# An S5 stage in another order, a layer-vector schedule with one knot moved, and two norm transposes one step earlier

## What is computed

```
def s5_mixer(h, w_in, ..., d_skip, w_glu):
    u = h @ w_in
    bu_r, bu_i = (u by group) @ bbr, (u by group) @ bbi
    _, _, s_r, s_i = associative_scan(combine, (a_r, a_i, bu_r, bu_i), axis=0)
    y = s_r @ c_re - s_i @ c_im + d_skip * u
    ya, yb = split(gelu(y) @ w_glu, 2)
    return ya * sigmoid(yb)

for layer in range(2):            # second network
    mod = silu(c) @ ada_w[layer] + ada_b[layer]      # shifts, scales, gates
    h = rms_norm(x) * g * (1 + sc1) + sh1
    x = x + g1 * mixer(h)
    x = x + g2 * conv_ffn(rms_norm(x) * g * (1 + sc2) + sh2)
    (the same for ctx)
```

## Time and profile before

| | us |
|---|---|
| median of 3 runs | 3034.11 |
| lowest, highest | 3031.2, 3043.46 |
| the profiled execution | 3034.11 |
| its span in the profile | 3032.3 |
| TensorE busy | 2926.8 |
| VectorE busy | 1806.9 |
| ScalarE busy | 1103.4 |
| GpSimd busy | 407.0 |

### The profile page before, as it was taken

One profiled execution on the slowest core, in us unless ns is written; L12 is line 12 of the kernel. 1 busy time (PEld: TensorE's weight loads), 2 busy tenths in 40 slices (PEclk: granted clock), 3 DMA queues, 4 the chain that ended last, 5 costly groups with the idle time before them and its releaser, 6 DMA issues. The chain is left out here.

```text
span 3032.3 us, 37645 instructions
## 1 busy us (share of the span) xinstructions
PE 2926.8 (97%) x15078; PEld 2437.5 (80%) x15078; DVE 1806.9 (60%) x2518; ACT 1103.4 (36%) x1571; POOL 407.0 (13%) x390
## 2 busy tenths in 40 slices
PE   6999988999999999999999999999999999999999
PEld 5778767788878778888768888889998886778887
DVE  7456546766666567776536586665764437554443
ACT  3233224333332442323324432234553426442322
POOL 0100111686642100001000000000000103100000
PEclk9999999999999999999989999999999999999999
DMA  6444322455638555554314365544553431123232
GB/s 268 145 134 139 105 97 78 147 179 171 225 127 268 169 180 170 160 166 148 118 50 139 111 188 180 181 153 126 181 175 100 133 95 51 38 84 99 96 97 84
DMA packets 123310, 421.00 MB, mean 139 GB/s; under 512 B 21520, under 2 KB 21520, under 8 KB 122368
## 3 DMA queue, kind: packets, MB, share of 16 engines
q1 hardware_dynamic: 102096, 369.67, 37.9%
q0 software_dynamic: 11056, 41.95, 4.2%
q10 hardware_dynamic: 9984, 6.97, 0.7%
HBM read 401.31 MB, written 19.86 MB: 139 GB/s over the span
## 5 line engine op out<-in xcount | busy, mean ns | idle before, releaser
L121 DVE TENSOR_TENSOR wl<-raw,wh 128x1024 fp32r<-128x1024 f32 x506 | 659.9, 1305 | 545.0 <-ACT wh L118 519.0
L112 PE MATMUL bk<-HH,wh 128*128 128x512 f32 x2176 | 862.3, 396 | 25.2 <-DVE HL L133 13.4
L112 PE MATMUL bk<-HL,wh 128*128 128x512 f32 x2176 | 854.8, 393 | 0.0
L112 PE MATMUL bk<-HH,wl 128*128 128x512 f32 x2176 | 854.3, 393 | 0.0
L118 ACT ACTIVATE wh<-raw 128x1024 fp32r<-128x1024 f32 x506 | 531.1, 1051 | 428.5 <-PE bk L112 421.2
L112 PEld LDWEIGHTS bk<-HH,wh 128*128 128x128 f32 x2176 | 413.8, 190 | 119.5 <-DVE HL L133 16.0
L112 PEld LDWEIGHTS bk<-HH,wl 128*128 128x128 f32 x2176 | 413.3, 190 | 87.5
L112 PEld LDWEIGHTS bk<-HL,wh 128*128 128x128 f32 x2176 | 414.2, 190 | 85.6 <-issue 1.0
L124 DVE CUSTOM_DVE_ANT_0 ttr<-ar,cB 128x1024 f32<-128x1024 f32 x240 | 309.9, 1291 | 2.2
L112 PE MATMUL bk<-gh,wh 128*128 128x512 f32 x704 | 274.3, 390 | 0.3 <-DVE gl L121 0.3
L112 PE MATMUL bk<-gh,wl 128*128 128x512 f32 x704 | 273.9, 389 | 0.0
(11 more groups left out here) (301 smaller groups left out, 3863.3 us busy)
## 6 DMA issues: line engine op xcount, KB each, us to landing
raw<-in_wts_dram SPq DMA_DIRECT2D x506, 512.0 KB, 3.6
ar<-in_ada_dram SPq DMA_DIRECT2D x176, 512.0 KB, 4.2
first<-in_ada_dram SPq DMA_DIRECT2D x16, 512.0 KB, 15.3
F_d<-CA POOLq DMA_DIRECT2D x8, 512.0 KB, 5.0
E_d<-stg POOLq DMA_DIRECT2D x16, 256.0 KB, 4.1
M_d<-K_d POOLq DMA_DIRECT2D x8, 512.0 KB, 11.7
EB<-E_d POOLq DMA_DIRECT2D x8, 512.0 KB, 6.6
EB<-M_d POOLq DMA_DIRECT2D x8, 512.0 KB, 7.1
```

The lines of the kernel that those rows point to most:

```text
L112: return Nothing() if self.e is None else self.e.matmul(*a, **k)
L121: return Nothing() if self.e is None else self.e.tensor_tensor(*a, **k)
```

## The change

There are four edits.

1. In S5, PE runs all eight tiles of `s5u` before `past(1)`, where two of them stood behind `past(1)` and `own(1)`. `out(0)` moves ahead of `past(2)`, and `own(2)` and `out(1)` ahead of `past(3)`. `LOADS` and the places of the fetches follow. On DVE the `lo` of units 139 and 140, which stood behind `scan(1)` and `scan(3)`, now both stand ahead of `scan(1)`.
2. In `KNOTS` the point (142, 78) becomes (138, 78), so the ten modulation steps due by unit 152 start at unit 140.
3. In `f2` the PE transpose `norm_turn(cf2)` moves from the start of up 3 to the start of up 2.
4. The same in the context FFN for `norm_turn(o)`.

```
-KNOTS = (... (122, 78), (142, 78), (152, 88), ...)
+KNOTS = (... (122, 78), (138, 78), (152, 88), ...)

-LOADS = [E0, E1, M0, M1, E2, E3, M2, M3, E4, E5, F0, F1,
-         F2, F3, E6, E7, M4, M5, M6, M7, F4, F5, F6, F7]
+LOADS = [E0, E1, M0, M1, E2, E3, M2, M3, F0, F1, E4, E5,
+         M4, M5, F2, F3, E6, E7, M6, M7, F4, F5, F6, F7]

 s5_pe:
             own(0)
-            for _ in range(2):
-                next(g)
+            run(g)
             past(1)
             own(1)
-            run(g)
+            out(0)
             past(2)
-            out(0)
+            own(2)
             out(1)
             past(3)
-            own(2)
             own(3)

 s5_vec:
             lo(e, base["s5u"] + 5 + 3)
+            lo(e, base["s5u"] + 7 + 3)
             scan(1)
-            lo(e, base["s5u"] + 6 + 3)
             scan(2)
             scan(3)
-            lo(e, base["s5u"] + 7 + 3)

 s5_pool:
-                for qr in {5: (0, 1), 10: (2,), 15: (3,)}.get(n, ()):
+                for qr in {5: (0, 1), 9: (2,), 10: (3,)}.get(n, ()):

 tensor_program:
-            ffn_pe(e, f2, lambda e, *key: norm_turn(e, n_cf2, 4) if key == ("up", 3) else None)
+            ffn_pe(e, f2, lambda e, *key: norm_turn(e, n_cf2, 4) if key == ("up", 2) else None)
-            ffn_pe(e, fc, lambda e, *key: norm_turn(e, n_o, 5) if key == ("up", 3) else None)
+            ffn_pe(e, fc, lambda e, *key: norm_turn(e, n_o, 5) if key == ("up", 2) else None)
```

More of the change, by code:

```diff
@@ L362, in build @@
         mm_ = Space()
-        KNOTS = ((0, 0), (2, 16), (12, 24), (58, 48), (76, 48), (122, 78), (142, 78), (152, 88), (214, 132), (222, 132), (240, 144), (260, 144), (318, 192), (600, 192))
+        KNOTS = ((0, 0), (2, 16), (12, 24), (58, 48), (76, 48), (122, 78), (138, 78), (152, 88), (214, 132), (222, 132), (240, 144), (260, 144), (318, 192), (600, 192))
         def mod_rate(u):
@@ L1293, in build @@
         d_yf = [landing("yf") for _ in range(8)]
-        LOADS = [("E", 0), ("E", 1), ("M", 0), ("M", 1), ("E", 2), ("E", 3), ("M", 2), ("M", 3), ("E", 4), ("E", 5), ("F", 0), ("F", 1),
-                 ("F", 2), ("F", 3), ("E", 6), ("E", 7), ("M", 4), ("M", 5), ("M", 6), ("M", 7), ("F", 4), ("F", 5), ("F", 6), ("F", 7)]
+        LOADS = [("E", 0), ("E", 1), ("M", 0), ("M", 1), ("E", 2), ("E", 3), ("M", 2), ("M", 3), ("F", 0), ("F", 1), ("E", 4), ("E", 5),
+                 ("M", 4), ("M", 5), ("F", 2), ("F", 3), ("E", 6), ("E", 7), ("M", 6), ("M", 7), ("F", 4), ("F", 5), ("F", 6), ("F", 7)]
         SLOT = {kind: n % 5 for n, kind in enumerate(LOADS)}
```

## The result

| | before | after |
|---|---|---|
| median, first comparison (6 runs each) | 3042.37 us | 3060.23 us |
| ratio | | 1.0061 [1.0040, 1.0083] |
| median, repeated on another chip (23 and 6 runs) | 3040.93 us | 3054.02 us |
| ratio | | 1.0051 [1.0034, 1.0067] |
| profiled execution / its span | 3034.11 / 3032.3 us | 3058.09 / 3056.3 us |

The change is slower by 0.5 to 0.6%: +17.9 us between the medians of the first comparison, +13.1 in the second. The ratio is worked out from all runs and is not the quotient of the medians; by it the two differences are 18.6 and 15.5 us. The forecast was 3050.0 us with a range of 3041 to 3057, made as 3034.1 + 15.9. The direction was right and the time lies outside the range.

What follows compares the result with a forecast made beforehand. The prediction took TensorE, busy 2926.8 of 3032.3 us, as the bound. It added 5.6 + 2.6 + 3.0 + 2.2 + 2.5 = 15.9 us to 3034.1, giving 3050.0 us, range 3041 to 3057.

Steps and rivals of the forecast that it cites:

- The wait in the latent FFN, 5.6 us: Latent FFN, start of up 2: TensorE stands still 5.6 us at the moved transpose until DVE's reciprocal is made.
- 5.6 + 2.6 = 8.2: Latent FFN: the 5.6 us stall at the moved transpose plus 2.6 us for the clock drop behind it.
- The wait in the context FFN, 3.0 us: Context FFN, start of up 2: TensorE waits 3.0 us at the moved transpose for the reciprocal.
- Its clock loss, 2.2 us: Context FFN, behind the transpose's wait: a clock drop costing 2.2 us, with 0 and 2.9 as the ends.
- Rival D: Both FFNs: the moved transposes do not wait, so only S5's loss is left, 3036.6 us; chance 0.06.
- S5, +2.5 us: S5: old waits go, but later scans and a new 4.0 us wait ahead of `past(2)` net +2.5 us.
- E4: S5: the load `past(2)` waits for, landing at 958.6, 960.9 or 965.2; middle case a new 4.0 us wait.
- The knot, 0: The moved `KNOTS` point: modulation steps run earlier on DVE, mostly beside dense matmuls of `glu`, costed at 0.
- The base, 3034.1 us: Whole kernel before: the profiled execution's 3034.1 us, also the runs' median, to which the predicted loss was added.
- Rival A: Both FFN stalls come, but the clock holds once or S5 comes out even: 3045, or 3047 to 3048; chance 0.22.
- Rival B: S5 becomes bound by its loads, +7 us there in place of +2.5: 3054.5 us; chance 0.12.
- Rival C: Not slower: the S5 order's 7.4 us gain pays for the two stalls' 8.6, giving +1.2 or 3035; chance 0.06.

Runs made afterwards that it cites:

- s5_warm2: Kernel before with only the new S5 order, plus 16, 4 and 10 useless matmuls ahead of `past(2)`, `own(2)` and `out(2)`: 3035.85 us, ratio 0.9989.
- no_knot: The changed kernel without the `KNOTS` edit, so the new S5 order and both moved transposes, against the kernel before: 3056.13 us, ratio 1.0051.
- old_warm10: Kernel before, old S5 order, with ten useless 512-column matmuls put ahead of `past(3)`: 3040.02 us against 3040.4, ratio 0.9990.
- turn_cf2: Kernel before with only the context FFN's transpose moved to the start of up 2: 3043.17 us against 3040.93, ratio 1.0006.
- s5_warm: Kernel before with only the new S5 order, plus 16 useless 512-column matmuls ahead of `past(2)`: 3037.38 us, ratio 0.9999.
- knot: Kernel before with only the `KNOTS` point moved, S5 order and transposes as before: 3042.35 us, ratio 0.9997.
- old_warm: Kernel before, old S5 order, with twenty useless 512-column matmuls put ahead of `past(3)`: 3032.26 us against 3040.93, ratio 0.9978.

## Why the forecast was wrong, step by step

*The wait in the latent FFN, 5.6 us:* right. It is 5.45, by the row named in the forecast, and 8.6 us with its clock loss, where 5.6 + 2.6 = 8.2 was said. In the traces the two come to 8.4, and the second drop behind the norm sums, 1.5 us that the forecast did not have, comes on top.

*The wait in the context FFN, 3.0 us:* right, 2.92. *Its clock loss, 2.2 us:* wrong in after, where PEclk stays at 1.00 behind this wait, which the forecast had named as a sign against itself; 1.7 us in the profile of edit 4 alone. Edits 3 and 4 cost 12.2 us by the runs where the forecast has 13.4, so the sum is nearer than its terms. Rival D is excluded.

*S5, +2.5 us:* the pieces were right: scan 1 at 951.2 (said 952.9), a wait ahead of `past(2)` of 3.63 us (said 4.0), the reason E4. That `z(3)` ends at 983.37 in `s5_warm2` (said 983.5) is partly luck, as scan 1 starts 1.4 us earlier there and 1.4 us of idle time come between the scans. (One reading is 0.1 us off: 955.00 + 1.06 - 953.36 is 2.7 and not 2.8.)

Wrong was the clock. The forecast read from the earlier trace rows that it loses 2.2 us behind a wait and is back within 4 to 6 us. In S5 the pieces behind the wait are small matmuls, and half clock lasted 17 to 48 us in the profiles of the new order without filler, and 34 to 37.5 in five of six of the old one. So `glu` starts at 996.72, where the forecast had `out(3)` end between 987 and 991. As a difference the term need not be wrong, since both orders lose the clock. In the traces S5 takes 10.5 us more in after than in before. Against the five other profiles of the old order (mean 199.9) the two of the change are 1.4 and 5.3 us longer. With the 12.2 us of edits 3 and 4 that is 13.6 to 17.5, near the 15.5 and 18.6 that the ratios give.

*The knot, 0:* right, 3042.35 against 3042.19, and `no_knot` no better than the change.

*The base, 3034.1 us:* this is the step that failed. It was the profiled execution and the median of three runs, of which one was 3043.46. In the comparison itself the median of before is 3042.37, and in four later ones it is 3040.4 to 3042.2. Of the 10.2 us by which 3050.0 missed 3060.2, 8.3 are the base and 2.0 the difference (17.9 against 15.9). The cause is the clock reading above: the forecast took a stage with 6.8 us at half clock as what before always does. The forecast's difference of 15.9 us, a ratio of 1.0052, lies in both measured intervals; put on 3041 to 3042 it gives 3057 to 3058. That this difference fits so well is partly luck: terms that were too high (the second clock loss) and one that was missing (the drop behind the norm sums) offset each other. What was missing is the question why the three runs were 12 us apart (3031.2 to 3043.46); the profiles of the old S5 order differ by 8 to 10 us in the length of that stage alone. The range should have taken in a base of up to 3043.

Rival A has the right pieces (the second drop partly absent), but not S5. Rival B said that E4 to M7 would hold S5 for 7 us; S5 lost more than that in the traces, but by clock: the waits there, 3.63 and 2.25 us, are 5.9 us up to the first matmul of `glu`, against the 5.2 us of before (0.72 + 3.00 + 1.43). Rival C needed scan 1 before 945, and it started at 951.2.

The Trainium skill, page "TensorE: Matmul & The Clock Gate", "Part 1: The HAM clock gate", says that the gate follows how busy TensorE has been lately, and that the same kernel can spend a different number of matmuls at the lower clock from run to run. It says the second of the start of a kernel. The traces here show the like in the middle of one (6.8 or 34 to 37 us in the same S5 order). The forecast did not draw on it.

What stays open: why small matmuls, with TensorE busy without a gap, leave the clock at 1.2 GHz for 47.8 us in one execution (the second profile of the change, with no wait behind 958.83) and for 6.8 us in another. In S5 every drop began at or behind a wait, and filling the wait took it away in most executions; the drop behind the norm sums had no wait ahead of it, so a wait is not needed everywhere. What decides the length is not shown, nor whether it is the missing idle time or the kind of work in the filler that helps. For that reason it stays open too whether edit 1 is worth anything: alone its median lay 5.2 us below before, by the ratio 3.0 [0.9979, 1.0000], and beside edits 3 and 4 (1.0051 without the knot, 1.0040 for the two edits alone) nothing of it is seen. The intervals allow both.

## What to carry to other kernels

Before a difference of 0.5% is forecast, find out what the spread of the kernel before is made of; one profile shows one course of it, and a stage with short matmuls behind a wait is where the courses part. A wait on TensorE is best priced by what follows it. In this kernel 5.45 us in front of 512-column matmuls cost its length and 3 us, 2.9 us in front of 256-column ones its length and 0 to 1.7 us, and waits in front of 64-column ones led in most executions to a stage 8 to 10 us longer. Where such a wait cannot be taken away, useless dense matmuls in its place can pay (0.9978 here), if they last until everything that is waited for has come; ten in place of twenty gave nothing that can be told from zero.

## What the runs showed of the hardware

- Single waits of 2.31 us (`old_warm10`), 1.71 us (`turn_cf2`, at 964.40) and 2.91 us (`turn_cf2`, at 2109.11) on TensorE stood at the start of half clock in these profiles, and shorter ones among small matmuls did too (0.56 us ahead of the drop at 984.5 in `s5_warm2`, 0.34 and 0.85 us ahead of that at 980.5 in `s5_warm`); the 2.92 us wait in after did not.
- Half clock also came with no wait ahead of it: around 2105 in after, behind 24 matmuls of one column, after more than 330 us without idle time.
- TensorE at 15.00 of 15.00 us busy, with 64-column matmuls, had a granted clock of 0.50 for all of that window (`knot`, 971 to 986).
- Useless work of 4.6 us saved 6.7 us (`old_warm`), and half of it saved nothing that can be told from zero (`old_warm10`).
